# Interleaving the columns of a split matmul: the moving operand and PSUM in another order, stage by stage

## The reference, cut to what matters

```
z   = rmsnorm(x) @ w_in                          # 2048 -> 6208
y_a = mla(...) @ w_attn_br                       # stage YA   2048 -> 2048
y_p = pool(...) @ w_pool_br
x   = x + rmsnorm((sigmoid(ga)*y_a + sigmoid(gp)*y_p) @ w_mix_out)     # stage MIX
kv  = rmsnorm(mem) @ w_mem_kv                    # stage MKV  2048 -> 4096
q   = rmsnorm(x) @ w_mem_q                       # stage MQ
x   = x + rmsnorm(attention(q, kv) @ w_mem_o)    # stage MO
a   = conv(rmsnorm(x) @ w_ffn_in)                # stage FIN  2048 -> 11264
x   = x + rmsnorm((gelu(gate) * up) @ w_ffn_out) # stage FOUT 5632 -> 2048
```

## Time and profile before

| what | value |
|---|---|
| device time, median of two runs | 1823.87 us |
| the two runs | 1823.71 and 1824.02 us |
| span of the profiled execution | 1822.3 us |
| TensorE busy | 1810.9 us (99%), 8228 matmuls |
| VectorE, ScalarE busy | 1016.6 us (56%), 927.7 us (51%) |
| DMA | 330.69 MB, mean 181 GB/s |
| TensorE's granted clock, mean | 0.999 |

### The profile page before, as it was taken

The page is one execution under the profiler, slowest core; times in us unless marked ns, Lnnn a source line. Parts: engine busy times, 40 slices in busy tenths (PEclk is TensorE's granted clock), DMA queues, the critical chain, the costliest instruction groups (busy, mean ns, idle before and its releaser), DMA issues.

```text
span 1822.3 us, 24021 instructions
## 1 busy us (share of the span) xinstructions
PE 1810.9 (99%) x8228; PEld 1483.6 (81%) x8228; DVE 1016.6 (56%) x1416; ACT 927.7 (51%) x1269; POOL 60.5 (3%) x132
## 2 busy tenths in 40 slices
PE   9999999999999999999999999999999999999998
PEld 7888888888887888888888878888888888888886
DVE  5554555555555554544444476666666666744444
ACT  7555556565546554544444464444444444443443
POOL 4000000000000200000000100000000000000000
PEclk9999999999999999999999999999999999999999
DMA  8465544455556655555444555555555555655553
GB/s 283 150 187 183 167 155 155 156 160 173 200 192 213 203 186 182 179 181 191 142 138 163 191 207 184 180 183 184 182 177 176 180 183 178 240 196 189 190 189 110
DMA packets 166408, 330.69 MB, mean 181 GB/s; under 512 B 7846, under 2 KB 13398, under 8 KB 164950
## 3 DMA queue, kind: packets, MB, share of 16 engines
q1 hardware_dynamic: 164806, 318.48, 53.1%
q10 hardware_dynamic: 1552, 11.54, 1.6%
HBM read 325.81 MB, written 4.19 MB: 181 GB/s over the span
## 4 chain that ended last, share of the span: by engine, by line
PE 98%; DVE 1%; ACT 0%; DMA 0%; issue 0%; SPq 0%; DVEq 0%; ACTq 0%
PE bank L454 30%; PE bank L456 30%; PE bank L455 30%; PE bank L841 1%; PE bank L486 1%; PE bank L770 1%; PE bank L787 1%; PE bank L653 1%; PE bank L652 1%; DMA bufX<-in_x 0%; PE bank L669 0%; PE bank L660 0%; DVE actA L1648 0%; PE bank L561 0%; PE bank L546 0%
## 5 line engine op out<-in xcount | busy, mean ns | idle before, releaser
L1348 DVE TENSOR_TENSOR wlo<-raw,whi 128x1024 fp32r<-128x1024 f32 x612 | 747.4, 1223 | 753.1 <-ACT whi L937 572.6
L937 ACT ACTIVATE whi<-raw 128x1024 fp32r<-128x1024 f32 x448 | 471.2, 1052 | 601.5 <-PE bank L456 601.4
L454 PE MATMUL bank<-whi,actA 128*128 128x512 f32 x1344 | 541.6, 403 | 1.3 <-DVE wlo L1348 0.5
L456 PE MATMUL bank<-whi,actA 128*128 128x512 f32 x1344 | 530.5, 395 | 0.0
L455 PE MATMUL bank<-wlo,actA 128*128 128x512 f32 x1344 | 530.2, 395 | 0.0
L456 PEld LDWEIGHTS bank<-whi,actA 128*128 128x128 f32 x1344 | 253.0, 188 | 59.4
L454 PEld LDWEIGHTS bank<-whi,actA 128*128 128x128 f32 x1344 | 253.1, 188 | 59.0 <-DVE wlo L1348 1.7
L455 PEld LDWEIGHTS bank<-wlo,actA 128*128 128x128 f32 x1344 | 253.3, 188 | 55.6
L923 ACT ACTIVATE whi<-raw 128x1024 fp32r<-128x1024 f32 (+1 forms) x164 | 168.7, 1032 | 172.5 <-PE bank L456 169.2
L454 PE MATMUL bank<-whi,actB 128*128 128x512 f32 x576 | 229.4, 398 | 0.0
L456 PE MATMUL bank<-whi,actB 128*128 128x512 f32 x576 | 227.4, 395 | 0.0
(11 more groups left out here) (215 smaller groups left out, 1212.4 us busy)
## 6 DMA issues: line engine op xcount, KB each, us to landing
raw<-in_w_ffn_in SPq DMA_DIRECT2D x88, 1024.0 KB
raw<-in_w_in SPq DMA_DIRECT2D x48, 1024.0 KB
raw<-in_w_mem_kv SPq DMA_DIRECT2D x32, 1024.0 KB
raw<-in_w_ffn_out SPq DMA_DIRECT2D x32, 1024.0 KB
raw<-in_w_attn_br SPq DMA_DIRECT2D x16, 1024.0 KB
raw<-in_w_mix_out SPq DMA_DIRECT2D x16, 1024.0 KB
raw<-in_w_mem_q SPq DMA_DIRECT2D x16, 1024.0 KB
raw<-in_w_mem_o SPq DMA_DIRECT2D x16, 1024.0 KB
```

The source lines that it names most:

```text
L454: pe.matmul(acc[t][:, 0:n], hi, wh, start=f, stop=False)
L456: mm = pe.matmul(acc[t][:, 0:n], lo, wh, start=False, stop=l)
L937: act.activation(whi[:, ks % AHEAD, 0:w], raw[:, c, ks % 2, 0:w], ACT.Copy).then_inc(hi_done, 1)
L1348: dve.tensor_tensor(wlo[:, vs % AHEAD, 0:w], raw[:, c, vs % 2, 0:w], f32(whi[:, vs % AHEAD, 0:w]), ALU.subtract).then_inc(lo_done, 1)
```

## The change

`half`, `unit` and `column` get an argument `order = (h, e)`. With it, the 512 columns of the moving operand and the 512 columns of the PSUM output are both walked in another order: the columns are seen as h equal parts, and the walk takes e neighbouring columns from part 0, e from part 1, and so on, and then the next e of each part. Source and destination have the same order, so every number lands at its old address. The stationary operand, the number of matmuls and of columns, the waits, the loads, ScalarE's and VectorE's instructions are as they were.

```diff
+        def lines(ap, order):
+            if order is None:
+                return ap
+            return ap.rearrange("p (h j e) -> p j h e", h=order[0], e=order[1])
...
-                wh, wl = whi[:, s, kk * n:(kk + 1) * n], wlo[:, s, kk * n:(kk + 1) * n]
+                wh, wl = (lines(w[:, s, kk * n:(kk + 1) * n], order) for w in (whi, wlo))
+                dst = lines(acc[t][:, 0:n], order)
-                pe.matmul(acc[t][:, 0:n], hi, wh, start=f, stop=False)
-                pe.matmul(acc[t][:, 0:n], hi, wl, start=False, stop=False)
-                mm = pe.matmul(acc[t][:, 0:n], lo, wh, start=False, stop=l)
+                pe.matmul(dst, hi, wh, start=f, stop=False)
+                pe.matmul(dst, hi, wl, start=False, stop=False)
+                mm = pe.matmul(dst, lo, wh, start=False, stop=l)
```

More of the change, by code:

```diff
@@ L444, in _, with half @@
     def _(pe):
-        def half(t, vs, lhs, kts, n, u, first, last):
+        def lines(ap, order):
+            if order is None:
+                return ap
+            return ap.rearrange("p (h j e) -> p j h e", h=order[0], e=order[1])
+        def half(t, vs, lhs, kts, n, u, first, last, order=None):
             s = vs % AHEAD
@@ L451, in half, with unit @@
                 hi, lo = lhs(0, k)[:, t * P:(t + 1) * P], lhs(1, k)[:, t * P:(t + 1) * P]
-                wh, wl = whi[:, s, kk * n:(kk + 1) * n], wlo[:, s, kk * n:(kk + 1) * n]
+                wh, wl = (lines(w[:, s, kk * n:(kk + 1) * n], order) for w in (whi, wlo))
+                dst = lines(acc[t][:, 0:n], order)
                 f, l = first and kk == 0, last and kk == len(kts) - 1
-                pe.matmul(acc[t][:, 0:n], hi, wh, start=f, stop=False)
-                pe.matmul(acc[t][:, 0:n], hi, wl, start=False, stop=False)
-                mm = pe.matmul(acc[t][:, 0:n], lo, wh, start=False, stop=l)
+                pe.matmul(dst, hi, wh, start=f, stop=False)
+                pe.matmul(dst, hi, wl, start=False, stop=False)
+                mm = pe.matmul(dst, lo, wh, start=False, stop=l)
             return mm
-        def unit(v, vs, lhs, kts, n, u, first, last):
+        def unit(v, vs, lhs, kts, n, u, first, last, order=None):
             pe.wait_ge(lo_done, v + 1)
-            mm = half(0, vs, lhs, kts, n, u, first, last)
+            mm = half(0, vs, lhs, kts, n, u, first, last, order)
             if last:
                 mm.then_inc(acc0_ready, 1)
-            half(1, vs, lhs, kts, n, u, first, last).then_inc(w_used, 1)
+            half(1, vs, lhs, kts, n, u, first, last, order).then_inc(w_used, 1)
         def lhsA(part_, k):
@@ L673, in _, with column @@
                         mm.then_inc(t_filled, 1)
-        def column(v, u, lhs, job):
+        def column(v, u, lhs, job, order=None):
             for k in range(8):
-                unit(v + k, k, lhs, (2 * k, 2 * k + 1), NC, u, k == 0, k == 7)
+                unit(v + k, k, lhs, (2 * k, 2 * k + 1), NC, u, k == 0, k == 7, order)
                 job(k)
@@ L697, in ya_column @@
                     pe.wait_ge(t_out, T_O + 8)
-                unit(V_YA + 8 * n + k, k, lhs_o, (2 * k, 2 * k + 1), NC, U_YA + n, k == 0, k == 7)
+                unit(V_YA + 8 * n + k, k, lhs_o, (2 * k, 2 * k + 1), NC, U_YA + n, k == 0, k == 7, (2, 4))
                 job(k)
@@ L721, in _ @@
         with pe.Fori(2, ND) as n:
-            column(V_MIX + 8 * n, U_MIX + n, lhsA, nothing)
+            column(V_MIX + 8 * n, U_MIX + n, lhsA, nothing, (2, 16))
         def mk_job(n):
@@ L741, in _ @@
         with pe.Fori(1, ND) as n:
-            column(V_MKV + 8 * n, U_MKV + n, lhsB, mk_job(n - 1))
+            column(V_MKV + 8 * n, U_MKV + n, lhsB, mk_job(n - 1), (2, 2))
         def x2_job(k):
@@ L750, in _ @@
         with pe.Fori(ND + 1, 2 * ND) as n:
-            column(V_MKV + 8 * n, U_MKV + n, lhsB, nothing)
+            column(V_MKV + 8 * n, U_MKV + n, lhsB, nothing, (4, 4))
         def mem_head(n):
@@ L794, in _ @@
         with pe.Fori(1, ND) as n:
-            column(V_MQ + 8 * n, U_MQ + n, lhsA, mem_head(n - 1))
+            column(V_MQ + 8 * n, U_MQ + n, lhsA, mem_head(n - 1), (2, 32))
         pe.wait_ge(t_out, T_MOUT + 6)
@@ L806, in _ @@
         with pe.Fori(1, ND - 1) as n:
-            column(V_MO + 8 * n, U_MO + n, lhs_o, nothing)
+            column(V_MO + 8 * n, U_MO + n, lhs_o, nothing, (8, 4))
         def x3_fill(f):
@@ L886, in fout @@
                     pe.wait_ge(f_lo, 2 * NF)
-                unit(V_FOUT + 24 * n + k, k, lhsG, range(k0, k0 + kc), NC, U_FOUT + n, k == 0, k == 23)
+                unit(V_FOUT + 24 * n + k, k, lhsG, range(k0, k0 + kc), NC, U_FOUT + n, k == 0, k == 23,
+                     (2, 8) if not isinstance(n, int) else None)
                 k0 += kc
```

## The result

The changed kernel takes **1883.7 us** (two runs, 1883.6 and 1883.8), against 1823.9 us before: a ratio of 1.033, 95% interval 1.031 to 1.035. It is slower by 59.8 us.

A forecast was written before the change was run, and what follows sets the result against it. TensorE was taken to bound the kernel, busy 99%, at 232.4 ns a matmul. All terms were 0, so the span stayed at 1822.3 us; with runs' median 1.6 us above, 1824 us, range 1810 to 1885.

The forecast's parts named there:

- No added work: Whole kernel: same matmuls, columns, weight loads and waits, no queue gets another instruction; cost 0.
- no cost in the writes: PSUM output of the changed matmuls: by the 8-byte cacheline rule all seven orders are free, cost 0.
- none in the weight load: TensorE: the 188 ns load runs beside the previous matmul, hidden while matmul distance exceeds 188 ns; cost 0.
- Value taken: 0 for each of the seven orders: 2112 reordered matmuls: an interleaved column costs nothing extra, taken between bounds of -34 and +423 us.
- rival 3: MKV 1 to 3: only e = 2 pays, as line entries double; +31 or +57.8 us, to 1855 or 1882; chance 0.11.
- 2 us for each 100 matmuls: Any changed stretch: the forecast fails if it grows by more than this.
- rival 1: Changed matmuls: each jump between distant 64-byte blocks costs 0.48 ns; 78 us more, to 1902 us; chance 0.10.
- Rival 2: All changed matmuls: two slots per out-of-order column, PSUM pipeline falling out of step; +423 us, to 2247 us; chance 0.08.
- Rival 4: Changed matmuls: another walk meets less loss; at most -34 us, to 1790 us; chance 0.06 for over 9 us gain.
- Rival 5: Changed matmuls: interleaving is folded back to one run when built, so nothing changes; 1824 us; chance 0.02.
- The rule on lines of 16 bytes: SBUF reads: two hits on a 16-byte line suffice for full speed, so all seven orders are free; sum 0.
- The control: FOUT 1 and 2, taken as unchanged, should keep 122.7 us in the changed kernel's trace.

The follow-up runs named there:

- e2: Changed kernel with only PSUM written in the new orders, the moving operand read in plain order: 1823.5 us, ratio 1.000 to the kernel before.
- e7: Plain-order kernel with FIN's sixteen loop units writing PSUM alone in fourteen other orders and plain: 1823.3 us, one run.
- e6: Plain-order kernel with FIN's sixteen loop units in sixteen orders on both sides, stationary operand there 32 columns instead of 128: 1924.9 us, one run.
- e1_moving_only: Changed kernel with only the moving operand read in the new orders, PSUM written in plain order: 1883.5 us, ratio 1.033 to the kernel before.

## Why the prediction was right or wrong, point by point

- **What bounds the kernel: right.** TensorE's matmul distance sets the time, every ns goes to the end one to one, and the other engines had slack to spare. The seven changed stretches grew by 60.0 us and the time by 59.8. VectorE's and ScalarE's mean durations, 1222 and 1056 ns after against 1223 and 1052, stayed as the prediction said.
- **No added work, no cost in the writes, none in the weight load: right** (e2, e7, e6).
- **"Value taken: 0 for each of the seven orders": wrong.** This is the step that failed, and with it the forecast of 1824 us. The cost is above zero for all seven, from 5 ns (2, 32) to 95 ns (2, 2). The range held the time, but only just under its upper end of 1885 and by the part that was there for rival 3: that is luck. By the prediction's own sign, 2 us for each 100 matmuls, it failed in MKV 1 to 3 (9.6), MO (4.1) and MKV 5 to 7 (3.4). The argument for zero was that neither columns nor bytes change. What changed is how often a line is entered and in which order lines come, and the runs put all of the 60 us on that read (`e1_moving_only` 1883.5 us, `e2_psum_only` 1823.5). The rows had a hint: plain order loses 0.03 ns a column that plain float32 does not lose. I weighed that under rival 1 as a price for each jump, at 0.10; in hindsight, with the 216 ns of the repeated walks, it was a sign that plain order is already slowed by its read. It did not say which other walks would cost: all seven orders did, (64, 4) did not, and (32, 4) gained.
- **Rival 3 (only e = 2 pays): near in the total, wrong in the make-up.** Its upper price, 57.8 us for two slots a column, looks like the 59.8 measured, and that is chance: (2, 2) paid 27.6 us, close to its lower price (31 us), and the other six orders paid 32.4 us, where it had zero. Two slots a column is what (4, 2) and (128, 2) cost, orders that the change does not use.
- **Rival 1 (a jump between 64-byte blocks): right in kind, wrong in rule.** It gave 107, 46 and 15 ns for e = 2, 4, 8. Measured, by the medians: 95; 18, 37 and 42; 10 ns. It gave zero for e = 16 and 32, which lost 8 and 5 ns, and by it (32, 4) and (64, 4) would cost 46 ns, where they cost nothing. Its 78 us (79 with the right count for FOUT) is 19 too many.
- **Rival 2 (the write falls out of step): wrong.** PSUM alone is 1.000. The general rule of the Trainium skill, "PSUM — Partial Sum Buffer", section "Specifications (TRN2)", that any non-contiguous pattern slows matmuls, did not hold for the orders tried, which all keep pairs together (231 or 232 ns). The Trainium skill's other rule, "Advanced Engine Details and Errata", section "PSUM Cachelines" (two neighbouring elements are enough), agrees with every PSUM order tried here.
- **Rival 4 (a gain): wrong for these seven orders,** though its bound, 216 ns, was reached by walks that repeat columns, and a gain of 1.2% exists with (32, 4). Rival 5 is wrong for them: the matmuls of (2, 2) have a latency of 0.49 us where it was 0.39.
- **The rule on lines of 16 bytes** (the Trainium skill, "SBUF — State Buffer", section "Door 1: The DMA port swizzle") was applied badly. Its second half, that each crossing to another line pays, was left out, and the runs bear it out in part: 64 entries 216 ns, 128 entries 232, but 218 for pairs that go to and fro between neighbouring lines. Its first half, that two hits on a line are enough for full speed, fails here for float32r as soon as the lines are not neighbours: with two hits a line (2, 2) takes 329 ns and (128, 2) 453 against 232.
- **The control was none.** FOUT 1 and 2 were misread as unchanged. The condition `not isinstance(n, int)` has to be read against the loop: only a column inside a `Fori` has an `n` that is no integer.

## What to carry to other kernels

Leave the moving operand of float32r matmuls in whole, consecutive lines of 16 bytes: half-used lines of distant parts cost 41 to 110% (327 to 487 ns against 232), two interleaved parts with runs of 4 to 32 columns 2 to 8%, and four or eight parts with runs of 4 columns 16 to 20%. Interleave on the PSUM side instead, where orders that keep pairs of columns together were free. Add up whole units before an order is believed to be faster: the median of (8, 8) was 2% under plain order in a unit whose twelve matmuls took 1% longer, and the kernel that used it everywhere was 3% slower.

## What the runs showed of the hardware that was not expected

- The 232 ns of a plain float32r matmul of 512 columns are not the array's own pace. With fewer lines entered it takes 216 ns, at the same granted clock (1.00).
- Where whole lines are read straight on, 128 entries take 232 ns and 64 take 216: an estimate of 1.8 ns an entry (232 / 128), by which 64 entries are hidden under the 216. It does not carry over to pairs. Two alternating walks of pairs lose 95 ns for any D from 8 to 256 columns, and next to nothing for lines that are neighbours (218 ns for D = 4). No count of entries tried here gives both.
- The weight load that runs beside a matmul was not seen to disturb its read: 113 instead of 188 ns of load changed no median distance by more than 5 ns.
- The same matmul in (8, 8) settles into one of two patterns, 227 ns or a mean of about 247, and keeps it over many units and stages. What picks the pattern was not found; the unit, with its slot and product, does not decide it alone. Nor was it found why 4 and 8 parts of whole lines cost more than 2, and 32 less than none.
